# The opening of a diffusion backbone: tokens and parameters loaded by channel, squares added on VectorE, adaptive groups of two tiles each

## The chip, the cores and the metric

The kernel runs on one core of a Trainium2 chip. The metric is the device time in microseconds of one execution, of which the median of a few runs is given. Lower is better.

## What is computed

A backbone of two layers over 512 latent tokens and 256 context tokens, 1024 channels, float32. Layer 0 mixes tokens with a Conformer convolution module, layer 1 with bidirectional retention; each is followed by a gated convolutional FFN. Every sub-layer starts like this:

```python
def rmsnorm(x, g):
    x32 = x.astype(jnp.float32)
    y = x32 * lax.rsqrt(jnp.mean(x32 * x32, axis=-1, keepdims=True) + NORM_EPS)
    return (y * g.astype(jnp.float32)).astype(x.dtype)
...
mod_x = (silu_c @ ada_w[i] + ada_b[i])[:, None, :]       # 6 * 1024 numbers a layer
mod_c = (silu_cc @ ada_w[i] + ada_b[i])[None, None, :]
sx1, cx1, gx1, sx2, cx2, gx2 = jnp.split(mod_x, 6, axis=-1)
hx = modulate(rmsnorm(x, norm1_g[i]), sx1, cx1)          # h * (1 + scale) + shift
...
z = h @ pw1_w + pw1_b                                    # the first product of layer 0
a, g = jnp.split(z, 2, axis=-1)
u = a * jax.nn.sigmoid(g)
u = dwconv(u, dw_w, dw_b)                                # 31 taps
```

The change touches what stands before `z`: loading the tokens, the RMS factor of each token, the shift and scale from the adaptive weights `ada_w`, and the order in which the first 128 output channels of the value and of the gate half of `z` ("block 0") are summed up.

## The kernel before

Activations stand in SBUF channel by channel: `X[:, k, :]` holds channels 128k to 128k+127 on the partitions and the 768 tokens (512 latent, 256 context) along the free axis; there are eight such tiles, k = 0 to 7. A product with a weight matrix runs in three passes of reduced precision (`w_hi*H_hi`, `w_hi*H_lo`, `w_lo*H_hi`). For that every weight tile is rounded by ScalarE (`split_hi`) and its rest is taken by VectorE (`split_lo`, L1691); the same is done with the activations (`H_hi` by ScalarE in `first_hi`, L1319; `H_lo` by VectorE in `first_lo`, L1794). A k-step of a unit (128 output channels) is six matmuls: three over the 512 latent and three over the 256 context tokens. Unit 0 is block 0's gate half, unit 1 its value half.

The engines each run a list of instructions written out by hand, in order, and wait for one another on semaphores. The opening goes like this:

- SyncE issues 16 small parameter loads and the 128x128 identity, then five constants. ScalarE's queue issues the six token loads (512 KB each, token rows). GpSimd waits for the first two of them (L619), then issues the adaptive weight groups (`load_first`, L494; two loads of 1 MB each per group) and the first two weight tiles in the order group 0, group 1, unit 0, group 2, unit 1, and group 3 once the products of group 0 have freed its buffer.
- TensorE transposes the tokens into `X` by way of PSUM (`token_transposes`, L907; ScalarE copies them out, L1306), and the parameters (L918). VectorE takes the mean square of each token with batch-norm statistics (L1812, L1816), ScalarE the root (L1309), VectorE the reciprocal (L1823) and six diagonal tiles (L1827), and TensorE spreads the factors over the partitions with two matmuls with `mean_of`. When these are done (`rows_ready`) VectorE normalizes the tiles of `X` one after another (`normed_rows`, L1844).
- A group `m` of adaptive weights becomes shifts and scales in four steps: `ada_products(m)` on TensorE (16 matmul records; each needs both 1 MB loads), `ada_copy(m)` on ScalarE (L1291), `ada_transposes(m)` on TensorE (L896), `ada_sum` on VectorE (L1749). Groups 0 and 1 together hold the shift and the scale of tiles 0 to 3, groups 2 and 3 those of tiles 4 to 7. Two small VectorE instructions then make the gain (`first_modulation`, L1774 and L1776). VectorE applies it (`first_shifted`, L1786: two instructions a tile) and takes the rest of `H_hi`.

TensorE's list around block 0 is `ada_products(0)`, `ada_transposes(0)`, the two matmuls of `rows_ready`, `ada_products(1)`, `ada_transposes(1)`, and then k-steps 0 to 3 of unit 0 around `ada_products(2)`, k-steps 0 to 3 of unit 1 around `ada_products(3)`, k-steps 4 and 5 of unit 0, `ada_products(4)`, k-steps 6 and 7 of unit 0, k-steps 4 to 7 of unit 1, `ada_transposes(4)` and `ada_products(5)`.

SyncE loads a later group into the buffer of the one before it when that one's products have read it, and this is a wait in its list:

```python
for half in range(2):
    sp.wait_ge(ada_done, 2 * m - 1 + half)
```

After block 0 comes the depthwise convolution: for each of eight blocks VectorE multiplies the gated values (L1997 for the latent, L2000 for the context tokens) and then runs 29 tap instructions (L1892 to L1916), while TensorE makes the next block (`pw1_body`): `ada_transposes`, `ada_products`, unit 2b, `ada_transposes`, `ada_products`, unit 2b+1.

Of the kernel before, what the change touches and what calls it, by code (L numbers as in the profile page):

```python
# [25 lines left out]
ALU = mybir.AluOpType  # L26
ACT = mybir.ActivationFunctionType
# [52 lines left out]
S_XT = 0  # L80
S_PW1 = S_XT + 12
# [45 lines left out]
FIRST_GROUPS = [0, 2, 1, 3]  # L127
# [13 lines left out]
def backbone(nc, x, c, ctx_tok, c_ctx, ada_w, ada_b, norm1_g, norm2_g, pw1_w, pw1_b, dw_w, dw_b, ln_g, ln_b,  # L141
             pw2_w, pw2_b, ret_w_in, ret_w_out, decay_f, decay_b, gn_f, gn_b, ffn_w_in, ffn_dw_w, ffn_dw_b,
             ffn_w_out, final_g, eye, ages, tri_low, tri_up, rope_row, rope_col, token_cols, out_cols_major, out):
    with ExitStack() as stack:
# [37 lines left out]
        tok_mv = sb("tok_mv", [P, 6, 2])  # L182
# [109 lines left out]
        xin = conv[:, :, :].rearrange("p a b -> p (a b)")[:, 0:6 * D].rearrange("p (t d) -> p t d", t=6)  # L292
        prow = tmp[:, :, :].rearrange("p a b -> p (a b)")[:, 0:768].rearrange("p (a b) -> p a b", b=P)
# [4 lines left out]
        ps = stack.enter_context(nc.psum_tensor("ps", [P, 8, 512], F32))  # L298
        rstd_rows = ps[:, 3:5, :].rearrange("p a b -> p (a b)")[:, 0:TOK]
# [23 lines left out]
        par_rows = sem("par_rows")  # L323
        tap_rows = sem("tap_rows")
# [3 lines left out]
        tokens_in = [sem("tokens_in0"), sem("tokens_in1"), sem("tokens_in2")]  # L328
# [5 lines left out]
        par_T = sem("par_T")  # L334
        par_ready = sem("par_ready")
# [7 lines left out]
        xT_done = sem("xT_done")  # L343
        tok_stats = sem("tok_stats")
        tok_var = sem("tok_var")
# [102 lines left out]

        def conv_part(j, t):

            return conv[:, j, t * PART:(t + 1) * PART] if t < 2 else conv[:, j, CTX_OUT:OUTW]
# [38 lines left out]
        def load_first(eng, m, half):  # L490

            rows = slice(half * D // 2, (half + 1) * D // 2)
            g = FIRST_GROUPS[m]
            eng.dma_start(ada_first[m][half], ada_w[0][rows, g * GROUP * P:(g + 1) * GROUP * P]  # L494
                          .rearrange("(k p) n -> p k n", p=P)).then_inc(ada_first_in[m], 16)
# [6 lines left out]
        def _(sp):  # L502

            for n, (lo, rows, src) in enumerate([
                    (C_COL, 8, c.rearrange("b (t p) -> (b t) p", p=P)),
                    (C_COL + 8, 8, c_ctx.rearrange("(t p) -> t p", p=P)),
# [1971 lines left out]
```

## Time and profile before

| | |
|---|---|
| median of 3 runs | 1671.19 us (1670.49 to 1671.51) |
| the profiled execution: time, span | 1671.56 us, 1669.7 us |
| TensorE busy | 98% of the span |
| VectorE busy | 57% |
| ScalarE busy | 41% |
| moved by DMA | 165.65 MB |

The span is from the first to the last instruction of the profiled execution; its time is 1.86 us more. A busy share is an average over stages with different limits, so the stages have to be looked at one by one. Times in the rows are microseconds from the start of the span.

### The profile page before, as it was taken

Reading aid. Unit: us, or ns where it says so; the run is one execution under the profiler, and the core shown is the slowest. Engines: PE = TensorE matmul, PEld = TensorE weight load, DVE = VectorE, ACT = ScalarE, POOL = GpSimd, SP = SyncE. Lnnn points to the kernel's source line nnn. Section 1 sums busy time; section 2 is a strip of 40 time slices with the busy share of each in tenths; the row PEclk is TensorE's granted clock in tenths of the full one; section 3 lists DMA queues with packets and bytes.
Section 4 is the critical chain, followed back from the end, with each engine's and each line's share of the span. In section 5 each row is a group of like instructions: output and inputs, shape, how many; then the busy total and the mean of one; then the engine's idle time right before and its main releaser. Section 6 shows DMA issues by size and latency. Waiting matters only on the chain.

```text
span 1669.7 us, 25567 instructions
## 1 busy us (share of the span) xinstructions
PE 1641.5 (98%) x10040; PEld 1435.3 (86%) x10040; DVE 957.8 (57%) x1511; ACT 677.5 (41%) x1019; POOL 169.5 (10%) x180
## 2 busy tenths in 40 slices
PE   6999989999999999999999999999999999999998
PEld 4777758998888888888899999999999888888888
DVE  6899987763424342334368665656566754543445
ACT  4656667642323222223245333424144543333333
POOL 2488851000000000000000000000000000000000
PEclk9999999999999999999999999999999999999999
DMA  9777742221221212121113221312122324233321
GB/s 338 253 252 251 252 160 95 76 75 48 67 76 55 70 56 71 55 71 55 59 51 92 64 70 39 83 51 63 58 64 76 99 79 124 87 104 89 100 88 51
DMA packets 238543, 165.65 MB, mean 99 GB/s; under 512 B 5288, under 2 KB 214040, under 8 KB 238456
## 3 DMA queue, kind: packets, MB, share of 16 engines
q1 hardware_dynamic: 234600, 150.43, 29.8%
q0 software_dynamic: 2992, 10.88, 2.0%
q10 hardware_dynamic: 864, 3.15, 0.5%
q8 instruction: 59, 0.97, 0.3%
q14 instruction: 28, 0.23, 0.0%
HBM read 162.34 MB, written 2.10 MB: 98 GB/s over the span
## 4 chain that ended last, share of the span: by engine, by line
PE 82%; DVE 14%; ACT 3%; issue 1%; DMA 0%; ACTq 0%; DVEq 0%
PE ps L702 81%; DVE ps L1895 3%; DVE ps L1912 3%; DVE w_lo L1691 2%; DVE rstd L1697 1%; DVE H_lo L1732 1%; PE ps L907 0%; DVE tmp L1720 0%; DVE ps L1910 0%; ACT sq L1279 0%; DVE sq L1720 0%; ACT tmp L1279 0%; DVE rstd L1708 0%; ACT H_hi L1270 0%; DVE ps L1892 0%
## 5 line engine op out<-in xcount | busy, mean ns | idle before, releaser
L702 PE MATMUL ps<-H_hi,w_hi 128*128 128x512 f32 (+1 forms) x1712 | 583.3, 341 | 8.3 <-DVE H_lo L1794 5.0
L702 PE MATMUL ps<-H_lo,w_hi 128*128 128x512 f32 (+1 forms) x1712 | 578.8, 338 | 0.0
L702 PE MATMUL ps<-H_hi,w_lo 128*128 128x512 f32 (+1 forms) x1712 | 578.1, 338 | 0.0
L702 PEld LDWEIGHTS ps<-H_hi,w_hi 128*128 128x128 f32 x1712 | 324.8, 190 | 62.2 <-issue 24.4
L702 PEld LDWEIGHTS ps<-H_hi,w_lo 128*128 128x128 f32 x1712 | 324.8, 190 | 35.0
L702 PEld LDWEIGHTS ps<-H_lo,w_hi 128*128 128x128 f32 x1712 | 325.0, 190 | 34.3
L1691 DVE TENSOR_TENSOR w_lo<-w_raw,w_hi 128x1024 fp32r<-128x1024 f32 x208 | 255.0, 1238 | 108.0 <-ACT w_hi L1232 75.1
L702 PE MATMUL ps<-mid_hi,w_hi 128*128 128x512 f32 (+1 forms) x592 | 199.5, 337 | 0.6
L702 PE MATMUL ps<-mid_lo,w_hi 128*128 128x512 f32 (+1 forms) x592 | 198.3, 335 | 0.0
L702 PE MATMUL ps<-mid_hi,w_lo 128*128 128x512 f32 (+1 forms) x592 | 198.1, 335 | 0.0
L2228 DVE SCALAR_TENSOR_TENSOR tmp<-ps,par,tmp 128x511 f32<-128x511 f32 x66 | 41.6, 657 | 231.3 <-ACT tmp L1576 155.0
L702 PE MATMUL ps<-w_hi,H_hi 128*128 128x256 f32 x512 | 145.2, 284 | 0.2 <-DVE w_lo L1691 0.2
L702 PE MATMUL ps<-w_lo,H_hi 128*128 128x256 f32 x512 | 144.9, 283 | 0.0
L702 PE MATMUL ps<-w_hi,H_lo 128*128 128x256 f32 x512 | 144.9, 283 | 0.0
L1232 ACT ACTIVATE w_hi<-w_raw 128x1024 fp32r<-128x1024 f32 x128 | 132.7, 1050 | 19.5 <-PE ps L702 19.5
L1574 ACT ACTIVATE tmp<-ps,par 128x512 f32<-128x512 f32 x44 | 34.3, 779 | 239.4 <-PE ps L702 239.4
L702 PEld LDWEIGHTS ps<-mid_hi,w_hi 128*128 128x128 f32 x592 | 112.3, 190 | 14.0 <-ACT tmp L1418 2.5
L702 PEld LDWEIGHTS ps<-mid_hi,w_lo 128*128 128x128 f32 x592 | 112.3, 190 | 11.5
L702 PEld LDWEIGHTS ps<-mid_lo,w_hi 128*128 128x128 f32 x592 | 112.4, 190 | 11.3
L647 POOL TENSOR_TENSOR odd_row<-odd_row,prod 128x392 f32<-128x392 f32 x107 | 115.1, 1076 | 14.3
L2070 DVE TENSOR_TENSOR X<-X,tmp 128x768 f32 (+3 forms) x44 | 35.7, 812 | 132.0 <-ACT tmp L1418 132.0
L702 PEld LDWEIGHTS ps<-w_hi,H_hi 128*128 128x128 f32 x512 | 98.2, 192 | 0.7 <-issue 0.4
(278 smaller groups left out, 2097.2 us busy)
## 6 DMA issues: line engine op xcount, KB each, us to landing
w_raw<-in_ffn_w_in SPq DMA_DIRECT2D x88, 512.0 KB, 3.8
ada<-in_ada_w SPq DMA_DIRECT2D x40, 1024.0 KB, 6.3
w_raw<-in_ret_w_in SPq DMA_DIRECT2D x40, 512.0 KB, 3.9
w_raw<-in_ffn_w_out SPq DMA_DIRECT2D x32, 512.0 KB, 4.4
w_raw<-in_conv_pw_w SPq DMA_DIRECT2D x22, 512.0 KB, 8.7
w_raw<-in_ffn_w_out SPq DMA_DIRECT2D x16, 384.0 KB, 3.5
ada<-in_ada_w POOLq DMA_DIRECT2D x4, 1024.0 KB, 13.5
w_raw<-in_ret_w_out SPq DMA_DIRECT2D x8, 512.0 KB, 4.2
```

The source lines that it names most:

```text
L647: nc.gpsimd.tensor_tensor(row, row, prod[:, at % PROD_RING, 0:w], ALU.add).then_inc(prod_added, 1)
L702: return nc.tensor.matmul(o, a, b, start=first, stop=last, skip_group_check=True)
L1232: A(w_hi[:, r, :], w_raw[:, r, :], ACT.Copy).then_inc(hi_ready, 1)
L1574: a = A(tmp[:, q, LATS], bank(q, 1), ACT.Identity, scale=w1, bias=b)
L1691: v.tensor_tensor(w_lo[:, r, :], w_raw[:, r, :], w_hi[:, r, :].bitcast(F32), ALU.subtract) \
L1697: v.reciprocal(rstd[:, part(t)], rstd[:, part(t)]).then_inc(rstd_ready, 1)
L1732: o = v.scalar_tensor_tensor(dst, b, shift(norm, t, j), hi, ALU.add, ALU.subtract)
L1895: v.scalar_tensor_tensor(sum_acc, frm, w, sum_acc, ALU.mult, ALU.add).then_inc(tap_done, 1)
L1912: v.scalar_tensor_tensor(even_acc, frm, w, even_acc, ALU.mult, ALU.add).then_inc(tap_done, 1)
L2070: v.tensor_tensor(row, row, tmp[:, p, 0:w], ALU.add).then_inc(x_updated, 1)
L2228: v.scalar_tensor_tensor(t[:, t0 + 1:t0 + m], b[:, 0:m - 1], wt[0], t[:, t0 + 1:t0 + m], ALU.mult, ALU.add).then_inc(g_taps, 1)
```

## The change

The host hands the kernel arrays that are laid out otherwise, and the opening is rewritten around them.

- **Tokens and parameters.** `x_cols` is the token array by channel, so four loads of 786 KB put it straight into `X`; one load of 393 KB brings all parameters. All are issued by SyncE, parameters first, the identity after them. The token and parameter transposes, the copies out of PSUM and the statistics instructions are gone. GpSimd waits for the second of the four token loads.
- **Mean squares.** ScalarE squares the eight tiles, VectorE adds them (seven additions of 128x768), and six matmuls with one column of `mean_of` sum over the channels.
- **Adaptive groups.** The host reorders the columns of the first four groups: group m now holds shift and scale of tiles 2m and 2m+1. Every adaptive load reads 8 KB rows in place of 2 KB rows.
- **Order.** On TensorE `ada_products(0)` stands first, then the six sums, and groups and k-steps alternate. The weight tile of unit 0 is loaded between groups 0 and 1, that of unit 1 between groups 1 and 2.

```diff
+            sp.dma_start(par[:], params).then_inc(par_in, 16)
+            for n in range(KT // 2):
+                sp.dma_start(X[:, 2 * n:2 * n + 2, :], x_cols[:, 2 * n:2 * n + 2, :]).then_inc(x_in[n], 16)
+            sp.dma_start(ident[:], eye).then_inc(eye_in, 16)
...
-            pool.wait_ge(tokens_in[0], 32)
+            pool.wait_ge(x_in[1], 16)
...
             for m in range(2):
                 for half in range(2):
                     load_first(pool, m, half)
-            load_gate_or_value(0)
+                load_gate_or_value(m)
             for half in range(2):
                 load_first(pool, 2, half)
-            load_gate_or_value(1)
...
+            ada_products(0)
+            pe.wait_ge(x_added, KT - 1)
+            for t in range(6):
+                m = mm(tok_sums[:, t:t + 1], x_squares[:, t * P:(t + 1) * P], mean_of[:, 0:1], True, True)
+            m.then_inc(x_summed, 1)
             pe.wait_ge(eye_in, 16)
             ada_transposes(0)
             pe.wait_ge(diag_ready, 1)
             mm(ps[:, 3, :], mean_of[:], flat_sq[:, LATS], True, True)
             mm(ps[:, 4, 0:CTX], mean_of[:], flat_sq[:, CTXS], True, True).then_inc(rows_ready, 1)
-            ada_products(1)
-            ada_transposes(1)
...
-            first_block(0, 0, 1)
+            first_block(0, 0, 2)
+            ada_products(1)
+            ada_transposes(1)
+            first_block(1, 0, 2)
             ada_products(2)
-            first_block(0, 1, 3)
             ada_transposes(2)
-            first_block(0, 3, 4)
-            pe.wait_ge(par_ready, 2)
+            first_block(0, 2, 4)
+            first_block(1, 2, 4)
             ada_products(3)
-            first_block(1, 0, 1)
             ada_transposes(3)
-            first_block(1, 1, 4)
-            first_block(0, KT // 2, KT - 2)
+            first_block(0, 4, 6)
+            first_block(1, 4, 6)
+            first_block(0, 6, KT)
             ada_products(4)
-            first_block(0, KT - 2, KT)
-            first_block(1, KT // 2, KT)
+            first_block(1, 6, KT)
             ada_transposes(4)
             ada_products(5)
```

ScalarE's list becomes:

```diff
+            for k in range(KT):
+                act.wait_ge(x_in[k // 2], 16)
+                if k >= 4:
+                    act.wait_ge(x_added, max(k - 4, 1))
+                A(norm_buf[k % 4], X[:, k, :], ACT.Square).then_inc(x_squared, 1)
+            A(tok_std_row, eps[:, 0:1], ACT.Sqrt)
             ada_copy(0)
+            act.wait_ge(x_summed, 1)
+            A(tok_rstd[:], tok_sums, ACT.Sqrt, bias=eps[:, 0:1]).then_inc(tok_std, 1)
...
+            for m in range(FIRST_GROUPS):
+                if m:
+                    ada_copy(m)
+                if m < 2:
+                    split_hi(m, m)
+                for j in (2 * m, 2 * m + 1):
+                    first_hi(j)
```

VectorE's list from the diagonal tiles on becomes:

```diff
+            ada_sum(0, 0, 0)
+            first_modulation(0)
             dve.wait_ge(rows_ready, 1)
...
+            for m in range(FIRST_GROUPS):
+                normed_rows([2 * m, 2 * m + 1])
+                if m:
+                    ada_sum(m, 0, m)
+                    first_modulation(m)
+                if m < 2:
+                    first_shifted(2 * m)
+                    split_lo(m, m)
+                    first_lo(2 * m)
+                    first_tiles([2 * m + 1])
+                else:
+                    first_tiles([2 * m, 2 * m + 1])
             split_lo(2, 2)
             split_lo(3, 3)
```

Everything behind block 0 is left as it was, but for semaphore counts and the source of the adaptive loads.

## Rows read from the trace of the kernel before

**Rows 1.** The page, part 1: busy time of each engine, share of the span.

```profile
PE 1641.5 (98%) x10040; PEld 1435.3 (86%) x10040; DVE 957.8 (57%) x1511; ACT 677.5 (41%) x1019; POOL 169.5 (10%) x180
```

**Rows 2.** Stretches: length, then PE, PEld, DVE, ACT, POOL busy, PEclk, DMA share, GB/s.

```profile
0.00:6.00 6.00, 0.00 (x0) 0.00 (x0) 0.00 (x0) 0.00 (x0) 0.73 (x8) 1.00 0.64 230
6.00:18.00 12.00, 9.25 (x46) 7.54 (x46) 7.86 (x14) 8.52 (x14) 6.41 (x8) 1.00 1.04 382
31.40:58.80 27.40, 26.16 (x155) 18.15 (x156) 20.93 (x42) 13.83 (x21) 0.00 (x0) 0.94 0.96 312
58.80:80.80 22.00, 22.00 (x144) 16.59 (x143) 21.82 (x38) 12.94 (x23) 16.36 (x15) 1.00 0.75 240
```

**Rows 3.** The chain that ended last, opening: start, length, what.

```profile
22.57 1.54 PE ps L702 x4
...
24.23 3.56 DVE conv L1844 x4
...
31.47 7.00 PE ps L702 x34
...
48.73 10.02 PE ps L702 x61
58.77 0.68 DVE tmp L2000
```

**Rows 4.** DMA issues of short stretches, and GB/s of one of them.

```profile
ada<-in_ada_w POOLq DMA_DIRECT2D x1, 1024.0 KB, 11.0
...
ada<-in_ada_w SPq DMA_DIRECT2D x1, 1024.0 KB, 5.1
...
ada<-in_ada_w SPq DMA_DIRECT2D x1, 1024.0 KB, 7.6
...
46.00:47.00 1.00, 0.80 (x7) 1.00 1.06 412
```

**Rows 5.** Timeline of PE and SP, and one row of the last chain.

```profile
33.62 1.68 PE L702 MATMUL ps<-ada_half,silu_c 128*32 128x512 f32 x8
35.13 1.03 PE L702 MATMUL ps<-w_raw,silu_c 128*32 128x512 f32 x8
...
59.09 1.92 PE L702 MATMUL ps<-ada,silu_c 128*32 128x512 f32 x16
...
52.31 0.77 SPq L579 DMA_DIRECT2D ada<-in_ada_w  x1
...
1662.56 1.37 PE ps L702 x8
```

**Rows 6.** Timeline of ACT and DVE in the opening.

```profile
20.61 0.30 ACT L1309 ACTIVATE tok_rstd<-tok_mv,eps 128x6 f32<-128x6 f32 x1
...
36.24 0.60 ACT L1291 ACTIVATE rstd<-ps 128x512 f32<-128x512 f32 x1 [1.95 <-PE ps L702]
...
28.45 0.87 DVE L1786 TENSOR_SCALAR tmp<-conv,gain,mod 128x512 f32<-128x512 f32 x2
...
30.37 0.95 DVE L1794 TENSOR_TENSOR H_lo<-tmp,H_hi 128x768 fp32r<-128x768 f32 x1
...
43.52 0.19 DVE L1749 TENSOR_REDUCE mod<-ps 128x8 f32<-128x32 f32 x1 [2.43 <-PE ps L896]
...
44.16 1.65 DVE L1786 TENSOR_SCALAR tmp<-conv,gain,mod 128x512 f32<-128x512 f32 x4
```

**Rows 7.** PE in short stretches: length, PE busy, PEclk, DMA share, GB/s.

```profile
27.00:31.00 4.00, 0.60 (x4) 1.00 1.03 378
...
32.00:34.00 2.00, 2.00 (x10) 0.50 1.01 363
...
54.38:58.57 4.19, 4.19 (x27) 1.00 1.01 385
```

**Rows 8.** Timeline where block 1 is handed from TensorE to VectorE.

```profile
80.24 0.60 PE L896 MATMUL ps<-ident,tmp 128*128 128x128 f32 x4
...
80.59 0.63 DVE L2000 SCALAR_TENSOR_TENSOR sq<-ps,par,rstd 128x256 f32<-128x256 f32 x1
```

More of the change, by code:

```diff
@@ L490, in load_first @@
         def load_first(eng, m, half):
[L492 to L495, printed above, removed]
+            eng.dma_start(ada_first[m][half], ada_groups[m, half].rearrange("p (k n) -> p k n", n=GROUP * P)) \
+                .then_inc(ada_first_in[m], 16)
         def raw_loads(unit):
@@ L877, in ada_products @@
                     pe.wait_ge(ada_row_ready, m)
-                first = isinstance(m, int) and m < 4
+                first = isinstance(m, int) and m < FIRST_GROUPS
                 for half in range(2):
@@ L2428, in _, with laid_out, columns @@
             ffn(FFN1, S_FFN1, 1, False, X_FFN1)
-_INS = ["x", "c", "ctx", "c_ctx", "ada_w", "ada_b", "norm1_g", "norm2_g", "conv_pw1_w", "conv_pw1_b", "conv_dw_w",
-        "conv_dw_b", "conv_ln_g", "conv_ln_b", "conv_pw2_w", "conv_pw2_b", "ret_w_in", "ret_w_out", "ret_decay_f",
-        "ret_decay_b", "ret_gn_f", "ret_gn_b", "ffn_w_in", "ffn_dw_w", "ffn_dw_b", "ffn_w_out", "final_g"]
+_PLAIN = ["conv_pw1_w", "conv_pw2_w", "ret_w_in", "ret_w_out", "ret_decay_f", "ret_decay_b", "ret_gn_f", "ret_gn_b",
+          "ffn_w_in", "ffn_w_out"]
+def laid_out(inputs):
+    import numpy as np
+    def columns(name):
+        return np.asarray(inputs[name]).reshape(-1, P).T
+    params = np.zeros((P, 768), np.float32)
+    for at, name in ((ADA_B, "ada_b"), (NORM1, "norm1_g"), (NORM2, "norm2_g"), (PW1_B, "conv_pw1_b"), (DW_B, "conv_dw_b"),
+                     (LN_G, "conv_ln_g"), (LN_B, "conv_ln_b"), (PW2_B, "conv_pw2_b"), (FFN_DW_B, "ffn_dw_b"),
+                     (FINAL_G, "final_g"), (C_COL, "c"), (C_COL + KT, "c_ctx"), (DW_W, "conv_dw_w")):
+        rows = columns(name)
+        params[:, at:at + rows.shape[1]] = rows
+    taps = columns("ffn_dw_w").reshape(P, DEPTH, 3 * FT)
+    for layer in range(DEPTH):
+        params[:, FFN_DW_W + P * layer:FFN_DW_W + P * layer + 3 * FT] = taps[:, layer]
+    tokens = np.concatenate([np.asarray(inputs["x"])[0], np.asarray(inputs["ctx"])[0]])
+    x_cols = np.ascontiguousarray(tokens.reshape(TOK, KT, P).transpose(2, 1, 0))
+    w = np.asarray(inputs["ada_w"])
+    first = w[0][:, 0:2 * D].reshape(D, 2, FIRST_GROUPS, 2 * P).transpose(0, 2, 1, 3).reshape(D, 2 * D)
+    both = np.concatenate([first, w[0][:, 2 * D:], w[1]], axis=1)
+    groups = np.ascontiguousarray(both.reshape(2, KT // 2, P, 24, GROUP * P).transpose(3, 0, 2, 1, 4)
+                                  .reshape(24, 2, P, KT // 2 * GROUP * P))
+    return [("x_cols", x_cols), ("params", params), ("ada_groups", groups)]
 def shape_constants():
@@ L2468 @@
     arrays, args = {}, []
-    for name, a in [(n, _np.ascontiguousarray(inputs[n])) for n in _INS] + list(shape_constants().items()):
+    for name, a in laid_out(inputs) + [(n, _np.ascontiguousarray(inputs[n])) for n in _PLAIN] + list(shape_constants().items()):
         arrays[f"in_{name}"] = a
```

196 lines of the change are left out of this document (45 added, 151 removed).

## The prediction

> **What bounds the kernel now.** I read the busy shares first, then stretches of the opening, then the chain that ended last, then timelines of single engines. The page has TensorE at 98% [rows 1], which would let one think that only fewer matmuls help. The stretches say otherwise for the part that matters here. Before 31.4 us TensorE mostly waits. From 31.4 to 58.8 it is busy 26.16 of 27.40 us [rows 2]. From 58.8 on VectorE is the bound: 21.82 of 22.00 us, and so through all eight convolution blocks. VectorE's list there begins with the context product of block 0 at L2000, which starts at 58.77 [rows 3]. Whatever moves that start moves the rest of the program by as much, since no idle time of VectorE lies behind it to absorb it. So the question is when L2000 starts after the change, and whether block 1 is then in time.
>
> The chain through the opening [rows 3]: the two matmuls that spread the token factors (22.57, 1.54 us), four normalizations from 24.23 (0.89 us each), the first k-step at 31.47, and an unbroken TensorE run of 10.02 us from 48.73 to L2000. From 31.47 on TensorE idles only about 1.4 us, so block 0 costs work and not waits.
>
> **Part 1: when the factors are there.** The new TensorE list puts `ada_products(0)` first, which needs all 2.10 MB of group 0. I count bytes. By 6 us the DMA engines have moved 6 x 230 = 1.38 MB, after that 382 GB/s at a share of 1.04 [rows 2]: they are full. Ahead of group 0, or beside it on the other queue, stand the tokens (3.15 MB), the parameters (0.39) and constants (0.15). With group 0 that is 5.79 MB, so the landing is at 6 + 4.41/0.382 = 17.5 us. The row for the same load before: the second half, issued at 7.04, takes 11.0 us and lands at 18.0 [rows 4]. Bounds: the best microsecond of the opening, 412 GB/s [rows 4], gives 16.7; 0.5 MB of the weight tile queued behind it sharing the engines gives 18.8. I take 17.4. GpSimd's later start (second token load at about 7.6 in place of 6.0) costs nothing, since the SyncE queue keeps the engines full until past 9 us.
>
> The squares and additions are hidden. The last token load lands between 12 and 15 us; two squares and two additions of 128x768 follow it, priced by the normalizations of the same size (3.56/4 = 0.89 us each [rows 3]), so the sum is there by 17.7 while the products run to 20. If that cover went, each microsecond of delay would count fully.
>
> From 17.4: `ada_products(0)` has 16 records. Warm they take 1.92 us (row at 59.09); with a granted clock of 0.50 eight of them take 1.51 us, 33.62 to 35.13 [rows 5, 7]. TensorE will have done nothing before this, so I take the slow price, 3.0 us: 20.4. The six sums: eight records of the same one-column form take 1.37 us in the last stage [rows 5], so twelve take 2.05, between 1.5 and 3: 22.45. Root to first normalization took 24.23 - 20.61 = 3.62 us [rows 3, 6] through instructions that stay. So the first normalization starts at 26.1, against 24.23: **1.9 us later**. All that goes from the start (48 transposes, 12 copies, a table load) is off the path or replaced by the wait for group 0.
>
> By the Trainium skill, DMA: Bandwidth & Descriptors, section Bandwidth, the line rate is 436 GB/s, reached better with long transfers. By that rate group 0 would land at 16.1 by my estimate and the result would be 1.3 us lower; this trace shows 412 GB/s at best.
>
> **Part 2: from there to block 0.** The first k-step came 7.24 us after the first normalization. The new list has two normalizations ahead of it, not four (-1.78), and the modulation is done earlier (-0.63: 27.82 to 28.45). So tile 0 is ready and the first matmul starts at 26.1 + 4.8 = 30.9, a gain of 0.5. Tile 1 follows 1.8 us later, at 32.6 (shift 0.87, rest 0.95 [rows 6]). Then the list turns against itself, because VectorE cannot go on to tile 2 before group 1 is through TensorE, and group 1's products are queued behind both k-steps of unit 0, though their data lies ready since 24:
>
> - k-steps 0 and 1 of unit 0: clock 0.50 again, since TensorE has idled from 26 to 30.9, as it idled before 31.47 [rows 7]. k 0 latent 1.4 (twice two thirds of the warm k-step below), wait for tile 1 to 32.7, k 1 latent 1.4, context 1.3: 35.3.
> - `ada_products(1)` 1.85, copy 0.55 (0.60 with its handover [rows 6]), transposes 0.5: 38.2.
> - VectorE, idle since about 34.5: sum and modulation 0.64 (43.52 to 44.16 [rows 6]), shift 0.8, `split_lo(1)` 1.15: 40.85. Only then may unit 1 start, so TensorE idles 2.8 us.
> - k-steps 0 and 1 of unit 1: a warm k-step is 1.03 (TensorE did the last four of unit 1 between 54.38 and 58.57 [rows 7], the last 0.06 of it a transpose), so 2.06; `ada_products(2)` 1.85; copy and transposes 1.05: 45.95. VectorE has tile 3 done at 43.4 and two normalizations at 45.2, and has tiles 4 and 5 by 50.1.
> - k-steps 2 and 3 of both units 4.13, products 1.85, copy and transposes 1.05: 53.0. VectorE then needs 0.7 for the modulation and 3.45 (shifts 1.65 [rows 6], rests 1.8) for tiles 6 and 7: 57.15.
> - k-steps 4 and 5 of both units and 6 and 7 of unit 0: 6.2 to 59.2, no wait. `ada_products(4)` 1.85, last two k-steps 2.06: 63.1. L2000 starts at 63.25.
>
> That is **+4.5 us** against 58.77. Check by parts: start -0.5; products and transposes of group 1 now behind the first k-step, +2.4; waits 0.5 + 3 x 0.55 + 2.8 = 4.9 against 1.4 before, +3.5; slow clock about 0.9 less of it. Each copy is now exposed, because the transposes stand right behind the products where before k-steps stood between. The half rate is paid once in both kernels, if the 2.8 us idle does not bring it back; if it does, eight records and a few k-steps cost up to 1.75 more.
>
> The Trainium skill, TensorE: Matmul & The Clock Gate, section HAM oscillation, warns that idle gaps bring the array back to half rate, and speaks against this list. The trace agrees for one gap: after the idle stretch up to 31.47 the clock is 0.50 until 34 to 35 [rows 7]. By the rule a second such stretch would make my sum 1.75 us more.
>
> **Part 3: block 1.** SyncE loads a half of group 5 when the matching half of `ada_products(4)` is done. Before, the second half was issued at 52.31 and took 7.6 us, to 59.9 [rows 4, 5], and `ada_products(5)` began at 59.09 [rows 5]: just in time, with 6.9 us between the two products. The new list has only two k-steps and the transposes between them, 2.6 us. Issued at 61.05, the second half lands at 68.1 to 68.65 (7.1 for group 4's row, 7.6 for group 5's), the products end at 69.3 and not at 65.5: TensorE is 3.8 us late for units 2 and 3. VectorE has little slack: TensorE was through unit 3 at 80.24, and VectorE took its context product at 80.59 as its turn came [rows 8], 0.35 us later. So **+3.4 us** more, once: from block 1 on a block costs TensorE 21.7 and VectorE 22.3. If the DMA lands at the 5.1 us of the first half [rows 4], this is 1.0; if it is hidden, 0. I take 3.4, since both loads go through the same engines one after another as before. ScalarE waits for unit 2 too, so its products start later, which is inside VectorE's slack of 2.5 us for the next weight split.
>
> Nothing behind block 1 changes in work; the adaptive loads only have longer rows, and the DMA share is 0.75 there [rows 2].
>
> **Sum.** 4.5 + 3.4 = +7.9 us. The profiled execution took 1671.56 (span 1669.7 and 1.86 around it), so its like would be 1679.5; the median shown is 0.37 lower, 1679.1.
>
> **The rivals.**
> - *Hidden group 5* (only +4.5): speaks for it that 8 KB rows may land faster; against it, 7.6 us for the like. 1675.7. Chance 0.22.
> - *Clock falls again* in the 2.8 us gap, +1.75 on top: 1680.9. For it: the stretch 27 to 31 with 0.60 us of work was followed by clock 0.50 [rows 7]. Against it: that gap was longer, 3.9 us. Chance 0.08.
> - *The DMA engines move the long rows much faster* (the other side). Then group 0, tokens and group 5 all come early. With group 5 hidden, L2000 is G + 45.85, where G is the landing of group 0, so break-even is G = 12.9, that is 4.41 MB in 6.9 us, 640 GB/s; faster by 0.2% needs G = 9.6. At 12 us it would be 1670.3. No row is above 412. It could also come from a chain that I priced too dear by 5 us. Chance 0.06 for faster.
> - *No change*: half of the waits that I list are not there, for instance with the first products on a warm TensorE (-1.1), sums at 1.5 (-0.5), group 5 hidden and group 0 at 16.7 (-0.7): +2.2, and 1.5 less elsewhere. Chance 0.05.
>
> **How the numbers follow.** My forecast has 0.59. 0.2% is 3.3 us, about what a measurement of this kernel can tell from no change. Slower: 0.59 + 0.22 + 0.08 = 0.89; same 0.05; faster 0.06. Low end: +2.8 (the hidden rival with G at 16.7 and warm first products, 4.5 - 0.7 - 1.0) is 1674.0. High end: G at 18.8 (+1.4) and the clock (+1.75) on 1679.1 is 1682.3.
>
> **What the profile would show.** First `ada_products` starting at 17 to 18 us; first L1844 at 26; first k-step near 31; an idle stretch of some 3 us on TensorE, ended by a weight split, near 38 to 41; transposes waiting for ScalarE three times; L2000 at 63; `ada_products(5)` waiting for a DMA near 65 to 68; block 1's L2000 at 88 to 89. I am wrong if group 0 lands before 14, if the first k-step comes before 28, or if VectorE has idle time behind 65.

## The result, and the profile after

The changed kernel takes 1687.93 us (median of 4 runs, 1687.30 to 1689.76), the kernel before 1671.32 us on the same chip. The ratio is 1.0101, with an interval of 1.0088 to 1.0113: 16.6 us slower. The direction was as forecast. The size was not: 7.9 us were forecast, and the time lies 5.6 us above the upper end of the range. The profiled execution took 1687.3 us, its span is 1685.5 us, 15.8 more than before. It is the fastest of the four, and every run below has a trace of one execution only.

The page of the profile does not lead to the place. Busy times are hardly changed against [rows 1]:

```profile
PE 1638.9 (97%) x9998; PEld 1425.4 (85%) x9998; DVE 956.4 (57%) x1498; ACT 676.2 (40%) x1015; POOL 167.6 (10%) x180
```

Where the time went is read from TensorE's timeline up to the end of block 0 (start, length, instruction; in brackets the idle time before and what ended it). In the new kernel products and k-steps are at L679, transposes at L873, the normalizations of before's L1844 are at L1772, and L1997 and L2000 are now L1923 and L1926.

```profile
18.98 3.64 PE L679 MATMUL ps<-ada,silu_c 128*32 128x512 f32 x16 [18.98 <-DMA ada<-in_ada_groups]
22.55 2.72 PE L679 MATMUL ps<-mean_of,conv 128*128 128x1 f32 x12
...
27.22 2.93 PE L679 MATMUL ps<-sq,mean_of 128*128 128x512 f32 x4 [1.00 <-DVE sq L1762]
35.13 0.77 PE L679 MATMUL ps<-H_hi,w_hi 128*128 128x512 f32 x1 [4.98 <-DVE H_lo L1739]
...
39.67 2.90 PE L679 MATMUL ps<-ada_more,silu_c 128*32 128x512 f32 x16
43.30 0.66 PE L873 MATMUL ps<-ident,rstd 128*128 128x128 f32 x4 [0.73 <-ACT rstd L1243]
46.75 0.79 PE L679 MATMUL ps<-H_hi,w_hi 128*128 128x512 f32 x1 [2.79 <-DVE w_lo L1636]
...
50.88 1.56 PE L679 MATMUL ps<-ada_half,silu_c 128*32 128x512 f32 x8
52.27 1.03 PE L679 MATMUL ps<-w_raw,silu_c 128*32 128x512 f32 x8
...
58.80 1.92 PE L679 MATMUL ps<-ada,silu_c 128*32 128x512 f32 x16
...
74.43 1.06 PE L679 MATMUL ps<-ada,silu_c 128*32 128x512 f32 x8 [1.45 <-DMA ada<-in_ada_groups]
77.10 1.06 PE L679 MATMUL ps<-ada,silu_c 128*32 128x512 f32 x8 [1.60 <-DMA ada<-in_ada_groups]
```

Sixteen records of products take 3.64 us for group 0, 2.90 for group 1 and 1.92 for group 3. It is the same work at two rates, half rate and full rate, and group 1 has some of each. Of the waits, the 2.79 us ended by the weight split and the 0.73 us for each copy are those of the prediction. The last two rows are its two waits for group 5.

VectorE, in the same stretch:

```profile
30.26 1.82 DVE L1772 TENSOR_TENSOR conv<-X,ps 128x768 f32<-128x768 f32 x2 [2.59 <-PE ps L679]
...
44.06 0.19 DVE L1694 TENSOR_REDUCE mod<-ps 128x8 f32<-128x32 f32 x1 [5.58 <-PE ps L873]
...
73.30 1.10 DVE L1923 SCALAR_TENSOR_TENSOR tmp<-ps,par,rstd 128x512 f32<-128x512 f32 x1 [4.21 <-ACT rstd L1307]
74.25 0.64 DVE L1926 SCALAR_TENSOR_TENSOR tmp<-ps,par,rstd 128x256 f32<-128x256 f32 x1
...
97.60 0.66 DVE L1926 SCALAR_TENSOR_TENSOR sq<-ps,par,rstd 128x256 f32<-128x256 f32 x1 [1.42 <-PE ps L679]
```

The first normalization comes at 30.26, not 24.23 [rows 3]; block 1's context product at 97.60, not 80.59 [rows 8]. So 17.0 us are lost by there, and it is still 17.0 at the last convolution block (230.91 against 213.96). About 1.3 us come back behind that block, where VectorE waited 1.41 us for TensorE in the kernel before (up to 236.04; the granted clock had been 0.66 from 215 to 220, and is 1.00 here) and does not wait now.

The stretches of the load (length, PE, PEld, DVE, ACT and POOL busy, PEclk, DMA share, GB/s) show a hole:

```profile
0.00:6.00 6.00, 0.00 (x0) 0.00 (x0) 0.00 (x0) 1.60 (x3) 0.72 (x8) 1.00 0.70 253
6.00:18.00 12.00, 0.00 (x0) 0.00 (x0) 6.71 (x7) 7.79 (x10) 5.10 (x8) 1.00 0.90 358
8.00:11.00 3.00, 0.00 (x0) 0.00 (x0) 2.61 (x4) 2.68 (x4) 2.83 (x5) 1.00 1.00 411
11.00:13.00 2.00, 0.00 (x0) 0.00 (x0) 1.82 (x2) 1.68 (x3) 2.00 (x4) 1.00 0.37 82
13.00:18.00 5.00, 0.00 (x0) 0.00 (x0) 1.92 (x2) 1.75 (x3) 0.27 (x1) 1.00 1.00 417
```

SyncE's queue has run dry soon after 11, and the loads of GpSimd, which began to issue at 8.17, hardly move before about 12.8 (2 GB/s from 12.0 to 12.5, 288 from 12.9 to 13.1). TensorE has no record at all before 18. Both engines of the squares are within their cover: the seven additions end at 15.05, and the products to 22.5.

### The profile page after: what moved, and what is told of

Its sections match the earlier page's. It is cut to its first block, busy times and chain, and to the rows that moved or that the text cites. A ratio compares the mean times of both kernels' runs of the same rounds, so it can differ in the third digit from the quotient of the medians.

```text
span 1685.5 us, 25451 instructions
## 1 busy us (share of the span) xinstructions
PE 1638.9 (97%) x9998; PEld 1425.4 (85%) x9998; DVE 956.4 (57%) x1498; ACT 676.2 (40%) x1015; POOL 167.6 (10%) x180
## 4 chain that ended last, share of the span: by engine, by line
PE 77%; DVE 5%; ACT 2%; issue 0%; ACTq 0%
PE ps L679 77%; DVE rstd L1642 1%; DVE H_lo L1677 1%; DVE w_lo L1636 1%; DVE tmp L1665 1%; DVE sq L1665 0%; DVE rstd L1653 0%; ACT sq L1231 0%; ACT tmp L1231 0%; ACT H_hi L1222 0%; DVE X L2001 0%; DVE H_lo L1675 0%; ACT tmp L1363 0%; DVE conv L2123 0%; PE ps L1077 0%
## 5 line engine op out<-in xcount | busy, mean ns | idle before, releaser
L679 PE MATMUL ps<-H_hi,w_hi 128*128 128x512 f32 (+1 forms) x1712 | 584.5, 341 | 11.1 <-DVE H_lo L1739 5.0
L679 PE MATMUL ps<-H_lo,w_hi 128*128 128x512 f32 (+1 forms) x1712 | 579.8, 339 | 0.0
L679 PE MATMUL ps<-H_hi,w_lo 128*128 128x512 f32 (+1 forms) x1712 | 579.4, 338 | 0.0
L679 PEld LDWEIGHTS ps<-H_hi,w_hi 128*128 128x128 f32 x1712 | 325.6, 190 | 64.4 <-issue 18.2
L679 PEld LDWEIGHTS ps<-H_hi,w_lo 128*128 128x128 f32 x1712 | 325.6, 190 | 35.2
L679 PEld LDWEIGHTS ps<-H_lo,w_hi 128*128 128x128 f32 x1712 | 325.8, 190 | 34.6
L679 PE MATMUL ps<-mid_hi,w_hi 128*128 128x512 f32 (+1 forms) x592 | 199.5, 337 | 0.5
L679 PE MATMUL ps<-mid_hi,w_lo 128*128 128x512 f32 (+1 forms) x592 | 198.2, 335 | 0.0
L679 PE MATMUL ps<-mid_lo,w_hi 128*128 128x512 f32 (+1 forms) x592 | 198.2, 335 | 0.0
L679 PE MATMUL ps<-w_hi,H_hi 128*128 128x256 f32 x512 | 145.1, 283 | 0.3 <-DVE w_lo L1636 0.3
L679 PE MATMUL ps<-w_hi,H_lo 128*128 128x256 f32 x512 | 144.9, 283 | 0.0
L679 PE MATMUL ps<-w_lo,H_hi 128*128 128x256 f32 x512 | 144.8, 283 | 0.0
L679 PEld LDWEIGHTS ps<-mid_hi,w_hi 128*128 128x128 f32 x592 | 111.4, 188 | 15.5 <-ACT tmp L1363 2.4
L679 PEld LDWEIGHTS ps<-mid_lo,w_hi 128*128 128x128 f32 x592 | 111.4, 188 | 13.1
L679 PEld LDWEIGHTS ps<-mid_hi,w_lo 128*128 128x128 f32 x592 | 111.2, 188 | 13.0
L624 POOL TENSOR_TENSOR odd_row<-odd_row,prod 128x392 f32<-128x392 f32 x107 | 115.0, 1075 | 15.5 <-ACT prod L1297 1.3
L679 PEld LDWEIGHTS ps<-w_hi,H_hi 128*128 128x128 f32 x512 | 98.2, 192 | 0.7 <-issue 0.4
```

Of the source, the lines that this page charges most:

```text
L624: nc.gpsimd.tensor_tensor(row, row, prod[:, at % PROD_RING, 0:w], ALU.add).then_inc(prod_added, 1)
L679: return nc.tensor.matmul(o, a, b, start=first, stop=last, skip_group_check=True)
```

## The experiments

Each was timed beside the kernel before on the same chip (1670.9 to 1671.5 us there); "the changed kernel" is the 1687.93 of above. In those that add matmuls, nothing reads what these write. A rate is read from the length of a known group: sixteen records of products take 1.92 us at full rate and 3.64 at half rate.

**e1_busy_start: TensorE kept busy while it waits for group 0.**

```diff
+            pe.wait_ge(x_in[3], 16)
+            for _ in range(24):
+                mm(ps[:, 2, 0:P], mean_of[:], mean_of[:], True, True)
             ada_products(0)
```

> 24 matmuls of mean_of with itself into an unused PSUM bank are put ahead of the first adaptive products, after the last token load; their result is not used. Theory A (half the surplus over my forecast is TensorE at half rate, since the changed list leaves it idle until 19 us): group 0's products take 1.9 to 2.0 us in place of 3.6, the six sums 1.4 to 2.0 in place of 2.7, the two spreading matmuls 1.5 in place of 2.9; the first normalization starts at 26.5 to 27.5 in place of 30.3, and the time falls by 3 to 4 us to about 1684. Theory B (these matmuls are slow for another reason, such as operands that arrive late): the extra matmuls change no duration behind them and the time stays at 1687 to 1689.

Measured: 1685.87 us (1683.72 to 1686.80), ratio 1.0083 [1.0066, 1.0100]. The three costs have their full-rate size:

```profile
20.88 1.92 PE L679 MATMUL ps<-ada,silu_c 128*32 128x512 f32 x16
22.73 1.50 PE L679 MATMUL ps<-mean_of,conv 128*128 128x1 f32 x12
...
26.19 1.56 PE L679 MATMUL ps<-sq,mean_of 128*128 128x512 f32 x4 [1.46 <-DVE sq L1769]
```

The added matmuls ran until 20.88, past the landing of group 0 (about 19.2), and the first normalization still came at 27.86, 2.4 us earlier. The time fell by 2.1 us and not by the 3 to 4 of theory A. From the first k-step on, rates were mixed again: a k-step of unit 1 began at full rate at 43.78 and fell to half by 45.1. It fell once more at the waits for group 5 (1.67 and 2.29 us), whose second half took 1.94 us for eight records, where full rate is 1.06.

**e2_busy_all: also before the first k-step of each unit.** e1 and

```diff
+            keep_busy(20)
             first_block(0, 0, 2)
             ada_products(1)
             ada_transposes(1)
+            keep_busy(11)
             first_block(1, 0, 2)
```

> As the run with extra matmuls at the start, and also 20 of them ahead of unit 0's first k-step and 11 ahead of unit 1's, where TensorE is idle 4.9 and 2.8 us. Theory A: all of block 0 then runs at full rate; a k-step pair of unit 1 takes 2.1 in place of 4.1, group 1's products 1.9 in place of 2.9, and together with the start the time falls by 7 to 9 us to 1679 to 1681, which is near my forecast of 1679.1. If only the waits matter (theory B): no change, or a loss of up to 1 us where the extra matmuls run past the moment at which the k-step could start.

Measured: 1680.17 us (1679.64 to 1683.21), ratio 1.0058 [1.0041, 1.0074], 7.8 us under the changed kernel with the order of its computation untouched.

```profile
24.32 1.56 PE L679 MATMUL ps<-sq,mean_of 128*128 128x512 f32 x4 [1.46 <-DVE sq L1771]
25.71 4.63 PE L679 MATMUL ps<-mean_of 128*128 128x128 f32 x40
30.86 0.47 PE L679 MATMUL ps<-H_hi,w_hi 128*128 128x512 f32 x1 [0.52 <-DVE H_lo L1748]
...
34.15 1.92 PE L679 MATMUL ps<-ada_more,silu_c 128*32 128x512 f32 x16
...
40.24 0.50 PE L679 MATMUL ps<-H_hi,w_hi 128*128 128x512 f32 x1 [0.33 <-DVE w_lo L1645]
...
65.52 1.07 PE L679 MATMUL ps<-ada,silu_c 128*32 128x512 f32 x8 [1.40 <-DMA ada<-in_ada_groups]
```

From 19 us to the end of block 0 at 63.52 every record is at full rate; from group 0's products to there it is 44.5 us, and 53.4 in the changed kernel. Behind the waits for group 5 the rate falls again: the granted clock is 0.50 from 70 to 73. VectorE's first normalization is at 25.98 and the first k-step at 30.86, where the prediction had 26.1 and 30.9. The forecast, 1679.1, fits this kernel and not the changed one.

**e3_group1_first: products and transposes of group 1 ahead of the first k-steps.**

```diff
-            first_block(0, 0, 2)
             ada_products(1)
             ada_transposes(1)
+            first_block(0, 0, 2)
             first_block(1, 0, 2)
```

> Only the order of TensorE's list is changed: group 1's products and transposes ahead of the first k-steps of unit 0. Theory A (VectorE waits for group 1, which is queued behind k-steps, and the idle gap of 2.8 us and one copy follow from it): the 5.6 us wait of VectorE for group 1 is gone, the gap ended by the weight split of unit 1 shrinks below 1 us, TensorE's work in that stretch moves into its own idle time, and the time falls by 6 to 9 us to 1679 to 1682. Theory B (group 1's weights land too late to be used there): the first k-step of unit 0 moves back by as much and the gain is under 2 us.

Measured: 1683.07 us (1681.98 to 1684.58), ratio 1.0069 [1.0052, 1.0085]. VectorE's 5.58 us wait for group 1 is gone. The wait for the weight split shrinks less than expected, to 1.66 us instead of 2.79:

```profile
39.72 0.80 PE L679 MATMUL ps<-H_hi,w_hi 128*128 128x512 f32 x1 [1.66 <-DVE w_lo L1636]
```

The time is 1 us above the expected range. Block 0's first product comes at 66.73, 6.6 us earlier, some 1.5 of it because the six sums ran at 1.50 us here. Of that, block 1 keeps half (94.16 against 97.60): the waits for group 5 are 2.35 and 1.30, and its second half ran at half rate, 1.94 for eight records.

**e4_pool_early: GpSimd waits for the first token load, not the second.**

```diff
-            pool.wait_ge(x_in[1], 16)
+            pool.wait_ge(x_in[0], 16)
```

> GpSimd waits for the first token load and not for the second before it issues the adaptive groups. Theory A (the DMA hole between 11 and 13 us, 121 and 43 GB/s, is GpSimd's delay from issue to first data): it issues at about 6.2 in place of 8.2, the hole closes, group 0 lands at 17 to 17.5 in place of 19.0 and the time falls by 1.5 to 2 us. Theory B (the hole has another cause, such as the additions of VectorE holding up the descriptors that GpSimd writes, since they run from 7.6 to 15 us): the first bytes of group 0 still come at about 13, and the time stays within 0.5 us; the token loads may even land later.

Measured: 1685.59 us (1684.74 to 1686.17), ratio 1.0087 [1.0070, 1.0104]. The hole is filled:

```profile
11.00:13.00 2.00, 0.00 (x0) 0.00 (x0) 1.79 (x3) 1.32 (x2) 1.35 (x3) 1.00 1.03 429
```

and yet group 0 comes only 0.9 us earlier, at 18.10, short of the expected 17 to 17.5. In this execution the parameters and tokens landed later than in the changed kernel's (193 GB/s up to 6 us, and 253 there), so GpSimd issued at 7.26 and not at 6.2. In e7, with the same edit, it issued at 6.10 and group 0 was there at 17.34, 1.6 us earlier. Group 0's bytes now move beside the tokens', and the last addition ends at 17.1 instead of 15.05. Theory B, that the additions hold up GpSimd's loads, does not fit: they run beside them here too. The other part of the gain is the clock's: group 1's products took 1.92 us and not 2.90, and nothing in the edit touches them.

**e5_gate_first: ScalarE takes block 0's sigmoids before the copy of group 4.**

```diff
-            ada_copy(4)
             act.wait_ge(h0_lo_ready, KT)
...
             gates(0)
+            ada_copy(4)
```

> ScalarE does block 0's two sigmoids ahead of the copy of group 4, for which it waits until 70.3 us in the changed kernel, 2 us after unit 0 was done. Theory A (what ends last is TensorE's arrival at block 1, set by the load of group 5): the first convolution block starts 1.0 us earlier (L1926 at 73.3 in place of 74.3) but VectorE then waits so much longer for block 1's context product, and the time stays within 1 us of 1687.9. Theory B (the late sigmoids are on the path): the time falls by 1 to 2 us to about 1686.5.

Measured: 1687.67 us (1687.15 to 1688.29), ratio 1.0103 [1.0086, 1.0119]. In the changed kernel ScalarE copies group 4 at 70.31 and only then loads the table for the sigmoids, which is what ends VectorE's 4.21 us wait at 73.30. Here VectorE begins block 0 at 69.43 as TensorE ends it. Its context product comes 0.57 us behind TensorE's last k-step and not 1.87, so the edit gives block 0 1.3 us; another 2.55 us come from the rates of this execution (the sums took 1.50 us). By block 1 all of it is lost: the context product there comes at 97.81 after a wait of 1.58 us for TensorE. The late sigmoids cost nothing that can be measured. The rate fell again at group 5:

```profile
74.70 1.94 PE L679 MATMUL ps<-ada,silu_c 128*32 128x512 f32 x8 [1.29 <-DMA ada<-in_ada_groups]
```

From this row's start to block 1's context product it is 23.1 us here, 22.7 in e1, 23.0 in e3 and 22.2 in e2, and 20.5 in the changed kernel's profile, in e4 and in e6. So in four profiles the waits for group 5 brought half rate back, and it cost 1.7 to 2.6 us there.

**e6_group4_earlier: `ada_products(4)` before the last two k-steps of unit 0.**

```diff
-            first_block(0, 6, KT)
             ada_products(4)
+            first_block(0, 6, KT)
             first_block(1, 6, KT)
```

> Group 4's products are moved ahead of k-steps 6 and 7 of unit 0, so that the load of group 5 into the same buffer starts 2 us earlier in TensorE's list. Theory A (the distance between group 4's and group 5's products is what makes block 1 late): the two DMA waits of 1.5 and 1.6 us ahead of unit 2 shrink to under 2 us together, block 1's context product starts 1.5 to 2.2 us earlier, and the time falls by 1.5 to 2.5 us to about 1686. Theory B (block 1 is late by what block 0 is late): no gain, since block 0's end does not move (L1926 within 0.5 us, or up to 1 us earlier by the sigmoids).

Measured: 1684.99 us (1683.48 to 1686.05), ratio 1.0083 [1.0066, 1.0100]. The waits for group 5 shrink from 1.45 and 1.60 to 0.79 and 1.27, and block 1's context product comes at 96.34, 1.3 us earlier. Half of that is the edit's: from block 0's context product to block 1's it is 22.76 us, and 23.35 in the changed kernel.

**e12_changed_group5_later: `ada_products(5)` not before unit 2 but behind its fourth k-step.**

```diff
             ada_transposes(4)
-            ada_products(5)
...
+                        if isinstance(i, int) and b == 1 and h == 0:
+                            unit_product(2, 2, KT, (H_hi, H_lo), streams, None, None, 0, 4)
+                            ada_products(5)
+                            k0 = 4
```

> The changed kernel with that move alone. Theory A: the two DMA waits of 1.45 and 1.60 us ahead of unit 2 go, VectorE's wait of 1.4 us for block 1's context product goes, and the time falls by 1.2 to 1.6 us to about 1686.4: that, and not 3.4 us, is what group 5 costs in the changed kernel beyond block 0's own lateness, since the late sigmoids already give block 1 about 2 us of slack. Theory B (the whole distance to group 5's landing counts): it falls by 3 us or more.

Measured: 1683.64 us (1683.28 to 1686.39, 5 runs), ratio 1.0082 [1.0068, 1.0096], 4.3 us under the changed kernel. The products of group 5 take an unbroken 1.92 us at 74.63 and VectorE does not wait at block 1 (93.03). From block 0's context product to block 1's it is 21.8 us, and 23.35 in the changed kernel: 1.5 us are the waits' own. The rest of the difference in the profile is an opening 3.0 us shorter (block 0's at 71.22, not 74.25), which this edit does not touch: there the six sums took 1.50 us and group 1's products 2.22. The same list of instructions ran at half rate for longer in one execution than in another. By the median alone theory B (3 us or more) would be right; the profile gives theory A's 1.5 us to the waits. What e12 also takes away is the occasion for the rate to fall there, which e5 prices at 1.7 to 2.6 us in those executions in which it does; how often it does in the changed kernel isn't known.

**e7_reordered: another order for groups and k-steps, with e4's wait and no added matmul.**

```diff
-            first_block(0, 0, 2)
             ada_products(1)
             ada_transposes(1)
-            first_block(1, 0, 2)
+            first_block(0, 0, 2)
             ada_products(2)
+            first_block(1, 0, 2)
             ada_transposes(2)
             first_block(0, 2, 4)
-            first_block(1, 2, 4)
             ada_products(3)
+            first_block(1, 2, 4)
             ada_transposes(3)
             first_block(0, 4, 6)
             first_block(1, 4, 6)
-            first_block(0, 6, KT)
             ada_products(4)
+            first_block(0, 6, KT)
             first_block(1, 6, KT)
```

> TensorE's list around block 0 reordered throughout: group 1's products and transposes ahead of the first k-step, then the products of group m+1 between the k-steps of the two units and its transposes behind them, so that ScalarE's copies are covered, and group 4 ahead of k-steps 6 and 7; GpSimd waits for the first token load. No extra matmuls. Theory A (waits made by the order, plus the half rate at the start): block 0's last k-step ends at 59 to 62 us in place of 72.3, and the time is 1674 to 1678. Theory B (order matters little, and the clock is all): 1682 to 1685, like group 1 first alone.

Measured: 1672.98 us (1671.79 to 1673.88, 10 runs), ratio 1.0013 [1.0003, 1.0022].

```profile
17.34 3.64 PE L679 MATMUL ps<-ada,silu_c 128*32 128x512 f32 x16 [17.34 <-DMA ada<-in_ada_groups]
20.91 2.72 PE L679 MATMUL ps<-mean_of,conv 128*128 128x1 f32 x12
...
25.58 2.93 PE L679 MATMUL ps<-sq,mean_of 128*128 128x512 f32 x4 [1.00 <-DVE sq L1762]
28.44 2.13 PE L679 MATMUL ps<-ada_more,silu_c 128*32 128x512 f32 x16
...
36.77 1.06 PE L679 MATMUL ps<-ada_half,silu_c 128*32 128x512 f32 x8
...
39.56 0.50 PE L679 MATMUL ps<-H_hi,w_hi 128*128 128x512 f32 x1 [0.87 <-DVE w_lo L1636]
```

The first three costs are as slow as in the changed kernel. But group 1's products stand directly behind the spreading, TensorE reaches full rate within them, and keeps it: the gaps of 4.98 and 2.79 us are now 0.75 and 0.87, and behind the longest that is left, 2.14 us ahead of the transposes of group 1, the products of group 2 still run at full rate. Order and the earlier issue together give back 15 of the 16.6 us. The earlier issue alone gave 2.3 (e4), and 1.6 us of group 0's landing; the order alone, without it, was not run. The time is better than theory A's 1674 to 1678.

**e8_reordered_busy and e9_reordered_18: e7 with added matmuls**, 24 after the last token load and 10 before the transposes of group 1 in e8, 18 after the third token load in e9.

```diff
+            pe.wait_ge(x_in[2], 16)
+            keep_busy(18)
             ada_products(0)
```

> As the reordered list, with 24 extra matmuls ahead of group 0's products and 10 behind group 1's (results unused). Theory A: the opening runs at full rate, the last k-step of block 0 ends at 56 to 58 us and the time is 1669 to 1672, level with the kernel before or up to 0.1% faster. Theory B (the clock costs nothing once the order is right): the same time as the reordered list without them.

> The reordered list with 18 extra matmuls ahead of group 0's products, started after the third token load so that they end before group 0 lands (24 of them, started after the fourth, ended at 21.95 us, some 3 us after it). Theory A (the half rate of the first products, sums and spreading matmuls, 3.6, 2.7 and 2.9 us in place of 1.9, 1.5 and 1.6, is on the path): the first normalization starts at 25 to 26.5 in place of 28.6 and the time is 1670 to 1671.5, 1.5 to 3 us under the reordered list alone. Theory B (that time is covered by later waits, such as the load of group 5): the same as the reordered list alone, 1672 to 1674.

Measured: e8 1673.5 us (1672.34 to 1676.91, 10 runs), ratio 1.0017 [1.0008, 1.0027]: its 24 matmuls ran until 21.95, past the landing, and in the profile the rate fell again behind the sums (spreading 2.93 us, group 1's products 3.48), so the first normalization came at 30.29, later than e7's 28.61. e9 1670.4 us (1668.56 to 1672.15, 11 runs), ratio 0.9994 [0.9985, 1.0003]. In e9 the first normalization is at 24.09 and block 0's context product at 56.30, 2.5 us earlier than before's 58.77. At block 1 nothing of it is left:

```profile
80.66 0.66 DVE L1933 SCALAR_TENSOR_TENSOR sq<-ps,par,rstd 128x256 f32<-128x256 f32 x1 [1.56 <-PE ps L679]
```

Before, it was 80.59 [rows 8]. The waits for group 5 stand in between: 0.48 and 1.63 us, and the second half runs slowly (1.77 for eight records). e11 asks whether they take the lead away.

**e11_group5_later: e9 with e12's move.**

> The reordered list with 18 extra matmuls, and group 5's products moved from the front of unit 2 to behind its fourth k-step, 4.2 us later in TensorE's list. Theory A (in the reordered kernel the start of block 1 at 80.7 is set by the load of group 5, since block 0 already ends 2.4 us earlier than in the kernel before and the rest is lost there): TensorE no longer waits 0.5 and 1.6 us for it, block 1's context product starts at 78.3 to 79, and the time is 1668 to 1669.5, faster than the kernel before by 0.1 to 0.2%. Theory B (block 1 is bound by TensorE's own work): the same 1670.4 as without the move.

Measured: 1669.62 us (1668.93 to 1671.97, 11 runs), ratio 0.9993 [0.9984, 1.0002]. The wait is gone and block 1's context product comes at 79.84, not at the expected 78.3 to 79: in this profile the rate fell behind the sums (spreading 2.93, group 1 3.52), and the first normalization slipped to 25.24. What a lead at full rate would give further stays open; nothing here beats the kernel before by what can be measured.

**e10_before_busy: the kernel before with 16 added matmuls in its 3.9 us of idle time before 31.47.**

```diff
+            for _ in range(16):
+                mm(ps[:, 2, 0:P], mean_of[:], mean_of[:], True, True)
             first_block(0, 0, 1)
```

> The kernel before, with 16 extra matmuls in TensorE's idle stretch ahead of the first k-step (27.6 to 31.5 us; results unused). Theory A (that idle stretch costs it the half rate until 35 us): the granted clock stays up from 31 to 35, the first k-step and group 2's products take half, block 0 ends 1.0 to 1.8 us earlier, and the time falls by up to 1.5 us unless the load of group 5, already just in time, takes it back. Theory B (the clock falls whatever TensorE does there, or block 1 is bound by that load alone): within 0.5 us of 1671.

Measured: 1669.86 us (1669.32 to 1672.13, 11 runs), ratio 0.9993 [0.9984, 1.0002]. The clock was 1.00 where [rows 7] has 0.50, and the same end came out (block 0's first product at 57.47, and at 57.44 in the kernel before):

```profile
39.89 1.92 PE L702 MATMUL ps<-ada,silu_c 128*32 128x512 f32 x16 [1.23 <-DMA ada<-in_ada_w]
```

TensorE was early and waited for group 3, whose products began at 39.88 before and at 39.89 here. So half rate is not a cost by itself: before, it lay beside a load; in the changed list it lay on the path.

## Why the prediction was wrong in size

The waits that the prediction names are there, one by one. The sum did not hold, and the miss can be laid out along TensorE's list until its last k-step of block 0, forecast at 63.1 and measured at 72.38. The forecast column is the prediction's. The measured one is read from the starts of the rows, products up to the start of ScalarE's copy.

| term | forecast | measured | miss |
|---|---|---|---|
| group 0 has landed | 17.4 | 18.98 | +1.6 |
| `ada_products(0)` | 3.0 | 3.57 | +0.6 |
| six sums | 2.05 | 2.76 | +0.7 |
| root to first normalization | 3.62 | 4.95 | +1.3 |
| from there to the first k-step | 4.8 | 4.87 | +0.1 |
| two k-steps of unit 0 | 4.4 | 4.54 | +0.1 |
| `ada_products(1)` | 1.85 | 2.98 | +1.1 |
| copy, transposes, wait for the split | 3.7 | 4.1 | +0.4 |
| two k-steps of unit 1 | 2.06 | 4.13 | +2.1 |
| `ada_products(2)` | 1.85 | 2.50 | +0.6 |
| the rest to the last k-step | 18.3 | 19.0 | +0.7 |

- **The step that failed is in Part 2: "The half rate is paid once in both kernels, if the 2.8 us idle does not bring it back".** The half rate that it pays once is that of `ada_products(0)` and of unit 0's first k-steps. The spreading (inside the root's row), groups 1 and 2 and the k-steps of unit 1 were priced by rows of a TensorE that had worked since 6 us, and the sums near such a price. "Before 31.4 us TensorE mostly waits" is a misreading that goes with it: it was busy 9.25 of 12 us in [rows 2], and 17.01 of 25.40 from 6 to 31.4. The changed list gives it nothing before 18.98, and then gaps of 1.00, 4.98 and 2.79 us. So half rate held from the first products until within `ada_products(1)`: with the too low price of `ada_products(0)`, +3.7. The transposes at 43.30 run at full rate (0.66; at 25.13 the same four took 1.09). Then it was half again: behind the 2.79 us gap the k-steps of unit 1 and half of group 2 cost +2.7.
- **That second part is the rival *clock falls again***, which had a chance of 0.08 and a price of 1.75. "That gap was longer, 3.9 us" was no argument against it. Together half rate is 6.4 of the 9.3 us. That it is the cause is shown by e2: useless matmuls in the gaps bring every row of block 0 to full rate, TensorE's stretch shrinks by 8.9 us (these 6.4 and about 2.3 that the forecast had already counted as half rate), and the time falls by 7.8.
- By the Trainium skill, TensorE: Matmul & The Clock Gate, section HAM oscillation, short bursts of matmuls with waits between them start at the slow clock again after each wait, and the remedy is an order that keeps them together. The trace agrees for the gap of 2.79 us, behind which two k-steps took 4.13 us and not 2.06, and not for every gap: behind 2.14 us in e7 and 1.45 and 1.60 us in the changed kernel the rows are at full rate.
- **Group 0's landing** was 1.6 us late, and that GpSimd's later start "costs nothing" is wrong: from its issue at 8.17 to the bytes it is some 4.6 us, and the queue ahead ended soon after 11. The 2 us at 82 GB/s are 1.6 us of loading at 411. The rate around the hole was higher than the 382 GB/s assumed, but by 18.98 some 6.2 MB had moved (6 us at 253 GB/s, 12 at 358 and 0.98 at 355), 0.4 more than the 5.79 counted ahead: what is queued behind shared the engines. With GpSimd's issue at 6.10 (e7) group 0 is there at 17.34, and at 18.10 with 7.26 (e4).
- **Two other prices** were near: 2.79 us against 2.8 for the wait behind the first k-steps, and three transposes that wait 0.72 to 0.73 us for a copy, against 0.55. e3 shows that the place of group 1 makes 1.1 of the 2.79 us; 1.66 are left with group 1 in front. Two of the prediction's sums are off by 0.15 us (2.8 where 38.2 to 40.85 is 2.65, and 45.95 where the terms give 45.81), which changes nothing.
- **Group 5** was sized well on TensorE: "TensorE is 3.8 us late", and the two waits are 3.05. Block 1's product moved by 17.0 and TensorE's end of block 0 by 13.8 (72.38 against 58.57), a difference of 3.2 against 3.4 forecast. Counted from VectorE's start of block 0, as the prediction's sum does, it is 1.5: its context product had moved by 15.5 already, since it came later behind TensorE. e12 takes the waits away, 1.5 us by the distance between blocks; its 4.3 in all are not the waits' alone, and how much of the remainder is a different course of the clock stays open. What the prediction did not see is that these waits can themselves bring half rate back (e1, e2, e3 and e5).
- **Not foreseen:** ScalarE's copy of group 4 ahead of block 0's sigmoids makes VectorE's start of block 0 1.3 us later (1.87 us behind TensorE, and 0.57 in e5). e5 shows that it costs nothing, as TensorE sets block 1.
- **A sign of being wrong** was "if VectorE has idle time behind 65". It has (4.21 us up to 73.30, 1.42 up to 97.60), but the forecast itself had block 1 late by 3.4 us, so this sign could not tell right from wrong.
- That e2 comes out 1 us from the forecast is partly luck: its group 0 is 1.6 us later than forecast, its products and sums 1.6 us shorter, and its half rate behind group 5 is in no term.

What is settled: the opening is slower since group 1 stands behind k-steps that need nothing of it and the products of groups 2 and 3 leave no k-step beside their copies; the half rate that these waits and the idle start bring is about half of the loss (the 7.8 us of e2). The 8.7 us that are left in e2 against the kernel before on its chip are the waits and group 0's landing, and up to 1.7 us of them the half rate behind group 5. Nearly all of it goes with another order and GpSimd's earlier issue together (e7). In how many executions the rate falls at which gap isn't settled, and with it the split by terms: the table is that of one execution.

## What to carry to other kernels

Price a matmul by what TensorE does in the microseconds ahead of it in the new list, not by the row that the same matmul has in the old one; a step that empties TensorE's first microseconds or opens a gap can make its successors dearer by up to a factor of two (1.92 us became 3.64 here). After a wait is priced, ask whether the slow stretch lies on the path: here 7.8 us came back with useless matmuls in the changed kernel and nothing that can be measured in the kernel before. Put work that another engine needs next ahead of work that nobody waits for, and a k-step between every product and the transposes that wait for its copy.

## What the hardware showed beyond that

- The rate that a matmul gets varies between executions. With nothing changed ahead of them on TensorE, the six sums took 2.72 us in the changed kernel, e4, e6 and e7, and 1.50 in e3, e5 and e12, where group 0's products ahead of them had taken 3.19 to 3.41 us and not 3.64. The spreading matmuls behind them, after 1.00 to 1.46 us without work, took 2.93 in all seven: where the sums had been at full rate, the rate fell across this short gap. In e1, e2 and e9, with added matmuls at the start, the same gap of 1.46 us left them at 1.56. The Trainium skill, TensorE: Matmul & The Clock Gate, section What's actually happening, says as much of a start: the number of slow matmuls differs from run to run. These rows agree for the start. They show it for a fall too: behind the same 2.79 us the first k-step of unit 1 was slow at once in the changed kernel and e4 (0.79 and 0.77 us for its first record) and still at full rate in e1, e5, e6 and e12 (0.50), where the rate fell a little later.
- The granted clock of the rows is not enough to see the slow start. In the changed kernel it reads 1.00 up to 44 us, over products that take 3.64 us and k-steps at half rate. Only the fall behind it shows:

```profile
22.00:44.00 22.00, 15.19 (x56) 8.64 (x52) 10.05 (x21) 5.66 (x9) 0.53 (x1) 1.00 0.66 264
44.00:46.00 2.00, 0.00 (x0) 0.00 (x0) 1.83 (x6) 1.51 (x4) 0.00 (x0) 0.78 0.00 0
46.00:51.00 5.00, 4.25 (x16) 3.45 (x20) 4.97 (x7) 1.19 (x2) 0.00 (x0) 0.50 0.01 3
```

  The length of a known group, 1.92 or 3.64 us for sixteen records, tells the level (2.4 or 1.2 GHz) there.
- With tokens by channel and adaptive loads of 8 KB rows, the opening moved 411 to 429 GB/s over stretches of 2 to 5 us; 382 was its rate before [rows 2].
- A load issued by GpSimd on its empty queue at 8.17, with SyncE's queue full until about 11, had its bytes from some 4.6 us later on and landed after 8.1 us:

```profile
ada<-in_ada_groups POOLq DMA_DIRECT2D x1, 1024.0 KB, 8.1
```

  One by SyncE, at 69.44, landed after 4.9.
